# A long convolution by cosine and sine tables, split by the position modulo four instead of modulo two

## The chip, the core and the metric

The kernel runs on one core of a Trainium2 chip. Its engines work from queues of their own: TensorE (PE, the matrix products), VectorE (DVE), ScalarE (ACT), GpSimd (POOL) and SyncE (SP, which here issues the loads). They meet at semaphores. The metric is the device time of one execution in microseconds (us). Before the change it is 796.03 us, the median of 3 runs (793.9 to 798.8).

## The reference

One encoder layer on x (512 positions x 1024 channels): a mixer, a cross attention to 256 memory rows, and a mixture of 16 experts. The change is in the mixer, whose first half is a Hyena operator:

```python
def hyena_mixer(u, short_w, short_b, skip, k_f):       # u: 512 positions x 1536 channels
    u = conv_general_dilated(u, ...3 taps, per channel...) + short_b
    v, g1, g2 = jnp.split(u, 3, axis=-1)               # 512 channels each
    z = v
    for o, gate in enumerate((g1, g2)):
        zc = fft_long_conv(z, k_f[:, o]) + skip[o] * z
        z = gate * zc
    return z

def fft_long_conv(z, k_f):                             # z: 512 positions
    zf = jnp.fft.rfft(z, n=2 * L, axis=1)
    return jnp.fft.irfft(zf * k_f[None], n=2 * L, axis=1)[:, :L]

# in reference():
    h = rms_norm(x, norm_mix)
    u_hy, q, k, v = jnp.split(h @ w_in, split_at, axis=-1)
    k_f = hyena_filter_spectra(L, ...)                 # k2 / (sum |k2| + EPS), then rfft over 1024
    y_hy = hyena_mixer(u_hy, ..., k_f)
    y_at = gqa_mixer(q, k, v, ...)                     # 8 query heads, 2 key heads, rope
    y = concatenate([group_rms_norm(y_hy, ..., 8), group_rms_norm(y_at, ..., 8)])
    x = x + y @ w_out
```

## The kernel before

One program is written out by hand for each engine, in the order in which it runs; nothing reorders it. The stages: the filter of the convolution (a small network, then its spectra), the projections of x by `w_in`, the two convolutions, grouped attention in 32 steps with the end of the Hyena half between them, the output projection, the memory attention, and the experts.

**Products.** Where a product must be exact to nearly float32, both operands are split into a high and a low part (`_hi`, `_lo`), and PE makes three fast products (`hi*hi`, `hi*lo`, `lo*hi`). `chunk_jobs` (L1992) does so with the projections. The weights come in pieces of 512 KB: SP loads a piece into one of 3 slots (`w_raw`, `load_piece`) as soon as PE has used the piece three before it, ACT rounds it (`weight_hi`, L727, `w_hi`), and DVE takes the rest (`weight_lo`, L1165, `w_lo`). The chunks are `mk`, `mv` (memory keys and values), `v`, `g1`, `g2` (the three Hyena streams), `q` and `kv`, in that order.

**Transforms.** The spectrum of 512 positions zero-padded to 1024 is made by tables of cosines and sines. Positions of equal parity go through the same half-size table (`dft`), and even and odd results are then added and subtracted (`sums_and_differences`, L1242 and L1243). `spec_jobs` makes the spectra of the filters by full float32 products, `fwd_jobs` those of z by the three fast products, `inv_jobs` the way back by full float32 products, all with channels as the 512 columns of the spectra and time as the 512 columns (2 x 256) of the way back. So z is turned from channels-on-partitions to time-on-partitions by `z_jobs` (`zT`) before each convolution. `pointwise` (DVE) multiplies with the filter's spectrum: 20 operations on 128x512 for each half f of the spectrum and each order o. `skipped` (L1352) adds the skip term, scaled by the filter's l1 norm (`l1_norm`), and `gated` (L1359) multiplies with the gate. `outer_taps` (L1257 to L1260) and ACT's `centre_tap` (L739) make the 3-tap convolution.

**Fillers.** At five places PE makes products of the identity with itself, which nothing uses (`constant_products`, L1968), while it would wait for DVE or ACT.

**PSUM.** PE writes into 8 banks, and a bank is used again once its reader has freed it. `psum_jobs` lists all jobs in PE's order, and the banks are given out in turn.

**Order.** On PE: `filt(0)`, `mv`, spectra (order 0, with `filt(1)` between), `v`, spectra (order 1), `zT(0)`, `g1`, `fwd(0)`, `g2`, `inv(0)`, `zT(1)`, `fwd(1)`, `q`, `kv`, `inv(1)`, the keys' and first queries' transposes (`kT`, `qT`), and the scores of attention. On DVE, `weight_lo` calls stand between the operations of the stages.

Of the kernel before, what the change touches and what calls it, by code (L numbers as in the profile page):

```python
# [6 lines left out]
F32 = mybir.dt.float32  # L7
# [13 lines left out]
HALF = T // 2  # L21
NQ, NKV, HD = 8, 2, 64
# [37 lines left out]
GATED_STEP = 1  # L60
HN_STEPS = [8, 12]
MK_STEP = 9
# [5 lines left out]
FILL = [3, 3, 2, 2] + [1] * 6  # L68


def psum_jobs():
# [6 lines left out]
    def spec(o, f):  # L78
        return [("spec", o, f, c) for c in range(4)]
# [3 lines left out]
    jobs += spec(0, 0) + filt(1, (0, 1)) + spec(0, 1) + filt(1, (2, 3))  # L83
    jobs += [("u", c) for c in range(4)] + [("l1", 0)] + spec(1, 0) + spec(1, 1)
    jobs += [("zT", 0, k) for k in range(4)] + [("u", c) for c in range(4, 8)] + [("l1", 1)]
    for o in range(2):
        jobs += ([("zT", o, k) for k in range(4)] if o else []) + [("fwd", o, f, c) for f in range(2) for c in range(4)]
        jobs += [("u", c) for c in range(8, 12)] if o == 0 else [(key, i) for key in ("q", "kv") for i in range(TT)]
        jobs += [("inv", o, c) for c in range(CT)]
    jobs += [("kT", 0), ("kT", 1), ("qT", 0), ("qT", 1)]  # L90
    n = TT * NQ
    jobs += [("S", s) for s in range(AHEAD)]
    for s in range(-2, n):
# [12 lines left out]
        if s in HN_STEPS:  # L106
            jobs += [("hn", HN_STEPS.index(s))]
# [23 lines left out]
def build(nc, a, out, xn_dram, y_dram):  # L131
    with ExitStack() as ctx:
# [16 lines left out]
        rope_tmp = at("rope_tmp", 36, [P, 640])  # L149
# [15 lines left out]
        dft = at("dft", 104, [P, 2, 4, HALF])  # L165
        idft = at("idft", 112, [P, 2, 4, HALF])
        spec = at("spec", 120, [P, 2, 2, 4, CH])
        decay = at("decay", 152, [P, 4, CH])
        zt_hi = at("zt_hi", 152, [P, 4, CH], F32R)
        zt_lo = at("zt_lo", 32, [P, 4, CH], F32R)  # L170
        dft_hi = at("dft_hi", 24, [P, 2, 4, HALF], F32R)
        dft_lo = at("dft_lo", 104, [P, 2, 4, HALF], F32R)
        mk_sq = at("mk_sq", 160, [P, 512])
        q_sq = at("q_sq", 152, [P, TT, 512])
        ep = at("ep", 160, [P, 4, CH])
        mlp_arg = at("mlp_arg", 172, [FF, T])
        mlp_k = at("mlp_k", 174, [FF, T])
        l1sum = [at("l1sum0", 168, [P, CH]), at("l1sum1", 170, [P, CH])]
        fabs = [at("fabs0", 172, [P, 2, CH]), at("fabs1", 140, [P, 2, CH])]
        ab = at("ab", 168, [P, 4, CH])  # L180
        sum_diff0 = at("sum_diff0", 176, [P, 2, 4, CH])
        sum_diff = [sum_diff0, sum_diff1]
        sd = at("sd", 176, [P, 2, 4, CH])
        odd = at("odd", 192, [P, 2, CH])
# [4 lines left out]
        kT = at("kT", 88, [P, NKV, 2, T], F32R)  # L189
# [10 lines left out]
        inv_wide = at("inv_wide", 176, [P, TT, CT, 2, HD])  # L200
# [3 lines left out]
        y_sq = at("y_sq", 176, [P, CT, CH])  # L204
# [49 lines left out]
        blk = at("blk", 202, [P, P])  # L254
# [14 lines left out]
        for n, j in enumerate(jobs):  # L269
            if j[0] == "O":  # L270
                b = 6
            elif first_s < n < tail_s and j[0] in ("OT", "hn", "hr"):
                number[j] = len(number)
                b = 7
            elif j[0] == "gates":
# [38 lines left out]
        def open_bank(pe, job):  # L314

            b, use = place[job]
            if use:
# [3 lines left out]
                                          "dft", "idft", "x2", "g_moe", "wr")}  # L321
# [9 lines left out]
        s_skip = sem("skip_scaled")  # L331
# [20 lines left out]
        s_hrec = sem("hyena_inverse_ready")  # L352
        s_hwide = sem("hyena_inverse_wide")
# [7 lines left out]
        s_yh = sem("y_hyena_ready")  # L361
# [57 lines left out]
        def mat(name):  # L419
# [7 lines left out]
                  ("g2", w_in[:, :, 1024:1536], 2, [("u", c) for c in range(8, 12)]),  # L427
                  ("q", w_in[:, :, 1536:2048], 2, [("q", i) for i in range(TT)]),
                  ("kv", w_in[:, :, 2048:2304], 4, [("kv", i) for i in range(TT)]),
# [59 lines left out]
        def _(sp_):  # L489
# [21 lines left out]
            for n, m in ((1, ones), (2, blk), (3, tri)):  # L511
                sp_.dma_start(m[:], a["mats"][:, n, :]).then_inc(ld["mats"], 16)
# [155 lines left out]
        def _(act):  # L668
# [37 lines left out]
            def evac_odd(key):  # L706
                n = transforms.index(key)
                if n:
                    wait_freed(act, transforms[n - 1] + (1,))
# [1849 lines left out]
```

## Time and profile before

| | |
|---|---|
| median of 3 runs | 796.03 us (793.9 to 798.8) |
| the profiled execution, its span | 791.7 us |
| PE busy | 747.9 us, 94% of the span |
| DVE busy | 603.7 us, 76% |
| ACT busy | 461.6 us, 58% |
| share of the chain that ended last | PE 72%, DVE 15%, ACT 6% |
| filters, projections and convolutions | about 36 to 252 us |
| attention with the Hyena half's end | about 252 to 345 us |
| the rest (output projection, memory attention, experts) | 345 to 792 us |

The profiled execution has no time of its own beside its span; the median lies 4.3 us above the span. "Busy" is the time in which an engine had an instruction under way. PE's instructions overlap, so what one costs is read from the distance between two starts. A wait stands in square brackets behind the instruction that waited, with the engine that ended it.

### The profile page before, as it was taken

What the parts mean: (1) busy time and instruction counts of PE and PEld (TensorE: products, weight loads), DVE (VectorE), ACT (ScalarE), POOL (GpSimd) and SP (SyncE); (2) the same over time, 40 slices, a digit from 0 to 9 for tenths busy, and PEclk for the clock granted to TensorE, in tenths of its full rate; (3) what the DMA queues carried; (4) which work ended last, traced back from release to release, by engine and by line L of the source; (5) the groups of instructions that cost most, each with busy time, mean ns of one, the idle gap of its engine ahead of it and who ended that gap; (6) DMA issues with size and microseconds to landing.
All of it is one profiled execution on the core that took longest, in us unless ns stands there. A gap on an engine that the chain in (4) does not pass through costs nothing.

```text
span 791.7 us, 10886 instructions
## 1 busy us (share of the span) xinstructions
PE 747.9 (94%) x3680; PEld 607.8 (77%) x3680; DVE 603.7 (76%) x930; ACT 461.6 (58%) x689; POOL 78.0 (10%) x94
## 2 busy tenths in 40 slices
PE   5899999999999898889999999999999999999994
PEld 3664858788898787678787787888888888888882
DVE  5767482997799877835548568899899999999882
ACT  5952333131233988621559333787888888887782
POOL 0000000000000000000000001122222232222111
PEclk9999999999999999999999998999999999999997
DMA  8830203020120200022130675999999999999741
GB/s 291 298 107 1 84 23 106 27 80 1 38 96 27 78 31 1 2 62 97 54 116 18 246 294 182 420 364 385 379 372 383 373 391 372 369 369 383 306 159 21
DMA packets 28542, 146.53 MB, mean 185 GB/s; under 512 B 4791, under 2 KB 6711, under 8 KB 21976
## 3 DMA queue, kind: packets, MB, share of 16 engines
q1 hardware_dynamic: 23320, 135.53, 45.3%
q0 software_dynamic: 5184, 10.50, 5.0%
q8 instruction: 23, 0.38, 0.2%
q14 instruction: 15, 0.12, 0.0%
HBM read 141.81 MB, written 12.58 MB: 195 GB/s over the span
## 4 chain that ended last, share of the span: by engine, by line
PE 72%; DVE 15%; ACT 6%; DMA 4%; issue 3%; SPq 0%; POOL 0%; DVEq 0%; ACTq 0%; POOLq 0%
PE bank L1992 17%; PE bank L2378 11%; PE bank L2380 10%; PE bank L2379 10%; PE bank L1930 9%; PE bank L1937 3%; DMA slot<-in_w_down 2%; PE bank L2373 2%; PE bank L2004 1%; ACT w_hi L727 1%; PE bank L2292 1%; PE bank L2290 1%; PE bank L2291 1%; DVE w_lo L1165 1%; PE bank L2415 1%
## 5 line engine op out<-in xcount | busy, mean ns | idle before, releaser
L1849 DVE TENSOR_TENSOR e_lo<-slot,e_hi 128x1024 fp32r<-128x1024 f32 x192 | 221.4, 1218 | 9.4 <-ACT e_hi L1045 9.3
L1045 ACT ACTIVATE e_hi<-slot 128x1024 fp32r<-128x1024 f32 x192 | 188.2, 1061 | 7.7 <-DMA slot<-in_w_down 4.9
L1165 DVE TENSOR_TENSOR w_lo<-w_raw,w_hi 128x1024 fp32r<-128x1024 f32 x41 | 49.4, 1222 | 69.8 <-ACT w_hi L727 69.6
L727 ACT ACTIVATE w_hi<-w_raw 128x1024 fp32r<-128x1024 f32 x41 | 42.7, 1057 | 96.9 <-DMA w_raw<-in_w_in 63.2
L2378 PE MATMUL bank<-e_hi,hgT_hi 128*128 128x512 f32 x240 | 95.0, 396 | 0.3 <-DVE hgT_lo L1861 0.3
L2380 PE MATMUL bank<-e_hi,hgT_lo 128*128 128x512 f32 x240 | 93.6, 390 | 0.0
L2379 PE MATMUL bank<-e_lo,hgT_hi 128*128 128x512 f32 x240 | 93.4, 389 | 0.0
L2378 PEld LDWEIGHTS bank<-e_hi,hgT_hi 128*128 128x128 f32 x240 | 45.2, 189 | 9.5 <-DVE hgT_lo L1861 0.7
L2380 PEld LDWEIGHTS bank<-e_hi,hgT_lo 128*128 128x128 f32 x240 | 45.1, 188 | 9.6
L2379 PEld LDWEIGHTS bank<-e_lo,hgT_hi 128*128 128x128 f32 x240 | 45.1, 188 | 8.9
L2378 PE MATMUL bank<-e_hi,gaT_hi 128*128 128x512 f32 x120 | 48.1, 401 | 0.0
L2380 PE MATMUL bank<-e_hi,gaT_lo 128*128 128x512 f32 x120 | 46.9, 391 | 0.0
L2379 PE MATMUL bank<-e_lo,gaT_hi 128*128 128x512 f32 x120 | 46.8, 390 | 0.0
L1992 PE MATMUL bank<-hT_hi,w_hi 128*128 128x512 f32 x96 | 37.9, 395 | 0.0
L1992 PE MATMUL bank<-hT_lo,w_hi 128*128 128x512 f32 x96 | 37.4, 389 | 0.0
L1992 PE MATMUL bank<-hT_hi,w_lo 128*128 128x512 f32 x96 | 37.4, 389 | 0.0
L1992 PE MATMUL bank<-w_hi,hT_hi 128*128 128x512 f32 (+1 forms) x96 | 34.0, 354 | 0.8 <-DVE hT_lo L1171 0.8
L1992 PE MATMUL bank<-w_hi,hT_lo 128*128 128x512 f32 (+1 forms) x96 | 34.0, 354 | 0.0
L1992 PE MATMUL bank<-w_lo,hT_hi 128*128 128x512 f32 (+1 forms) x96 | 34.0, 354 | 0.0
L1063 ACT ACTIVATE hgT_hi<-bank 128x512 fp32r<-128x512 f32 x28 | 15.2, 596 | 31.1 <-PE bank L2373 31.1
L636 POOL DMA_INDIRECT out_dram<-eo,meta_i x16 | 25.4, 1588 | 76.7 <-ACT eo L1080 46.4
L1937 PE MATMUL bank<-ident,pr 128*128 128x128 f32 x160 | 24.8, 277 | 8.1 <-ACT pr L891 6.3
(395 smaller groups left out, 1671.6 us busy)
## 6 DMA issues: line engine op xcount, KB each, us to landing
slot<-in_w_down SPq DMA_DIRECT2D x16, 2048.0 KB, 16.6
slot<-in_w_gate SPq DMA_DIRECT2D x16, 2048.0 KB, 14.6
slot<-in_w_up SPq DMA_DIRECT2D x16, 2048.0 KB, 16.0
w_raw<-in_w_in SPq DMA_DIRECT2D x18, 512.0 KB, 3.5
w_raw<-in_w_out SPq DMA_DIRECT2D x8, 512.0 KB, 3.7
w_raw<-in_w_k_mem SPq DMA_DIRECT2D x4, 512.0 KB, 6.1
x_in<-in_x SPq DMA_DIRECT2D x4, 512.0 KB, 9.2
w_raw<-in_w_v_mem SPq DMA_DIRECT2D x4, 512.0 KB, 6.0
```

The lines of the kernel that those rows point to most:

```text
L636: pool.indirect_dma_start(out[0], bass.IndirectOffsetOnAxis(ap=meta_i[:, q, 0:1], axis=0), eo[q][:], None, bounds_check=T - 1, oob_is_err= ...
L727: act.activation(w_hi[ring(m)][:], w_raw[ring(m)][:], ACT.Copy).then_inc(s_wh, 1)
L1045: act.activation(e_hi[buffer(b, j)][:], slot[slot_][:, 1024 * part:1024 * (part + 1)], ACT.Copy).then_inc(s_ehi, 1)
L1165: dve.tensor_tensor(w_lo[slot_][:], w_raw[slot_][:], w_hi[slot_][:].bitcast(F32), ALU.subtract)\
L1849: dve.tensor_tensor(e_lo[slot_][:, at_], slot[slot_][:, at_], e_hi[buffer(b, j)][:].bitcast(F32), ALU.subtract)\
L1930: ins = pe.matmul(dst, l, r, start=(n == 0), stop=(n == len(pairs) - 1))
L1937: ins = pe.transpose(bank(job)[:, n * width:(n + 1) * width], s, ident[:])
L1992: ins = pe.matmul(bank(job)[:, 0:width], left, right, start=(k == 0 and m == 0), stop=(final and m == 2))
L2373: ins = pe.transpose(banks[half][:, k * P:(k + 1) * P], hg[q][:, c:D:KT], ident[:])
L2378: pe.matmul(dst, act_hi, w_hi_, start=first, stop=False)
L2379: pe.matmul(dst, act_hi, w_lo_, start=False, stop=False)
L2380: return pe.matmul(dst, act_lo, w_hi_, start=False, stop=last)
```

## The change

The positions are taken modulo four. The four residues have tables of 128 x 128 (`dft`: residue r, cosine or sine), a spectrum of 512 bins is made of 4 x 128 by two levels of sums and differences, and one stage does half of the channels (h, 256 of 512) instead of half of the bins. For residues 1 and 3, PE itself adds and subtracts: both products go into one bank, for the difference with a negated table (`dft_neg`, `turn_hi`, `turn_lo`). So PE's products of the transforms have 256 columns each instead of 512, and there are half as many columns in all for the way back, three quarters for the spectra and for `fwd`.

The way back now gives time on partitions, for residues 2rp and 2rp+1 in one bank. z stays with time on partitions, so `zT(1)` falls away; instead the gates are turned (`gT`, by `gate_jobs`, 16 transposes for each order), and ACT copies them to `gateT`. The skip term is put into the filter before its spectrum (`skip_added`, on one row, behind a product `l1_row` that sums the l1 terms over the partitions), and 1/l1 is put into the taps of the gate (`gate_taps`), so `skipped` falls away and `gated` is one product. `g2` now comes last of the projections, the stages lie in another order, three of the five fillers are gone, and `STAGE_BANKS` gives these jobs fixed banks (`filt` has 4 of them). The end of the Hyena half in attention (`hn`, `hyena_inverse`, `hyena_norm`) is done by reductions over the free axis on DVE. The rope gains are multiplied into the rope tables once. What follows attention is unchanged.

```diff
+STAGE_BANKS = {"filt": lambda o, t, way: (2 * t + way) % 4, "mv": lambda j: 4 + j, "l1row": lambda o: 7, "l1": lambda o: 6 + o,
+               "spec": lambda o, h, r: 4 + SPEC_ORDER.index(r), "fwd": lambda o, h, r: 4 + SPEC_ORDER.index(r),
+               "u": lambda c: c % 4, "q": lambda i: i, "kv": lambda i: i, "zT": lambda r: r,
+               "gT": lambda o, r: 6 + r % 2, "inv": lambda o, h, rp: 4 + 2 * h + rp, "kT": lambda j: 6 + j, "qT": lambda h: 6 + h}
...
             for t in range(4):
                 filters(0, t)
             weight_lo(7, 1)
-            l1_add(0, 0)
-            l1_add(0, 1)
+            for t in range(4):
+                l1_add(0, t)
             weight_lo(8, 3)
-            l1_add(0, 2)
-            l1_add(0, 3)
-            spec_sums(0, 0)
+            skip_added(0)
+            butterfly(("spec", 0, 0), spec[:, 0, 0])
...
+            def butterfly(key, dst):
+
+                sums, turned = key + (1,), key + (3,)
+                if key[0] == "fwd" and key != ("fwd", 0, 0):
+                    dve.wait_ge(s_ab, 2 * key[1] + key[2])
+                even_sums(key)
+                a_, b_ = (halves(first_level[:, n, :]) for n in range(2))
+                wait_filled(dve, sums)
+                c_ = halves(bank(sums)[:])
+                dve.tensor_tensor(pair(dst, 0, 4), a_, c_, ALU.add)
+                free(dve.tensor_tensor(pair(dst, 2, 4), a_, c_, ALU.subtract), sums)
+                wait_filled(dve, turned)
+                d_ = halves(bank(turned)[:])
+                dve.tensor_tensor(pair(dst, 1, 6), b_, d_, ALU.add)
+                free(dve.tensor_tensor(pair(dst, 3, 2), b_, d_, ALU.subtract), turned)
...
+            def spectrum(o, h):
+
+                x, k_, low = second_level, spec[:, o, h], inv_in[h]
+                butterfly(("fwd", o, h), x)
+                if o:
+                    wait_filled(dve, ("inv", 0, h, 1))
+                products = first_level[:].rearrange("p (g n) w -> p (g n w)", g=1).rearrange("p (b n) -> p b n", n=HC)
+                same = dve.tensor_tensor(products, x[:], k_, ALU.mult)
+                dve.tensor_tensor(low[:, 0:4], x[:, 0:4], k_[:, 4:8], ALU.mult)
+                link(dve.tensor_tensor(low[:, 4:8], x[:, 4:8], k_[:, 0:4], ALU.mult))
+                return products
+
+            def filtered(o, h, products):
+
+                y, low = second_level, inv_in[h]
+                dve.tensor_tensor(y[:, 0:4], products[:, 0:4], products[:, 4:8], ALU.subtract)
+                link(dve.tensor_tensor(y[:, 4:8], low[:, 0:4], low[:, 4:8], ALU.add))
...
+                dve.tensor_tensor(c_, y1, y3, ALU.add)
+                swapped_difference(first_level[:, 3, :], y1, y3)
+                dve.tensor_tensor(a_, y0, y2, ALU.add)
+                link(dve.tensor_tensor(b_, y0, y2, ALU.subtract))
+                second_sums(low, (3, 2), (1, 6)).then_inc(s_ab, 1)
...
+            made = spectrum(0, 0)
+            weight_lo(15, 1)
+            filtered(0, 0, made)
+            weight_lo(16, 1)
+            made = spectrum(0, 1)
+            outer_taps(4)
+            weight_lo(17, 1)
+            filtered(0, 1, made)
+            gated(0, 0)
...
+            made = spectrum(1, 0)
+            weight_lo(19, 2)
+            filtered(1, 0, made)
+            for i in range(TT):
+                wait_freed(dve, ("q", i))
+            roped(0)
+            weight_lo(21, 1)
+            made = spectrum(1, 1)
+            weight_lo(22, 1)
+            filtered(1, 1, made)
+            roped(1)
+            weight_lo(23, 1)
...
+            fwd_jobs(0, 0)
+            main_chunk("g1", slice(0, 1))
+            fwd_jobs(0, 1)
+            main_chunk("g1", slice(1, 4))
+            inv_jobs(0, 0)
+            main_chunk("q", slice(0, 1))
+            gate_jobs(0)
+            main_chunk("q", slice(1, 2))
+            inv_jobs(0, 1)
+            fwd_jobs(1, 0)
+            main_chunk("q", slice(2, 3))
+            fwd_jobs(1, 1)
+            main_chunk("q", slice(3, 4))
+            main_chunk("kv")
+            main_chunk("g2")
+            inv_jobs(1, 0)
...
             for h in range(2):
                 qT_job(h)
...
+            gate_jobs(1)
+            inv_jobs(1, 1)
```

The first place is DVE's queue between the filter's l1 sums and the first sums of the filter's spectrum (`w_lo` is a low part of weights, `l1sum` and `fabs` the l1 sums, `first_level` and `spec` results of the sums). Before:

```order
L1165 TENSOR_TENSOR w_lo_54<-w_raw_50,w_hi_58 128x1024
L1218 TENSOR_TENSOR l1sum_93<-fabs_95 128x512
L1220 TENSOR_TENSOR fabs_96<-fabs_96 128x512
L1221 TENSOR_TENSOR l1sum_93<-l1sum_93,fabs_96 128x512
L1165 TENSOR_TENSOR w_lo_55<-w_raw_51,w_hi_59 128x1024
L1165 TENSOR_TENSOR w_lo_53<-w_raw_49,w_hi_57 128x1024
L1165 TENSOR_TENSOR w_lo_54<-w_raw_50,w_hi_58 128x1024
L1220 TENSOR_TENSOR fabs_95<-fabs_95 128x512
L1221 TENSOR_TENSOR l1sum_93<-l1sum_93,fabs_95 128x512
L1220 TENSOR_TENSOR fabs_96<-fabs_96 128x512
L1221 TENSOR_TENSOR l1sum_93<-l1sum_93,fabs_96 128x512
L1242 TENSOR_TENSOR spec<-bank,odd 128x512
```

And with the change:

```order
L1271 TENSOR_TENSOR fabs_95<-fabs_95 128x512
L1272 TENSOR_TENSOR l1sum_89<-l1sum_89,fabs_95 128x512
L1271 TENSOR_TENSOR fabs_94<-fabs_94 128x512
L1272 TENSOR_TENSOR l1sum_89<-l1sum_89,fabs_94 128x512
L1271 TENSOR_TENSOR fabs_95<-fabs_95 128x512
L1272 TENSOR_TENSOR l1sum_89<-l1sum_89,fabs_95 128x512
L1216 TENSOR_TENSOR w_lo_55<-w_raw_51,w_hi_59 128x1024
L1216 TENSOR_TENSOR w_lo_53<-w_raw_49,w_hi_57 128x1024
L1216 TENSOR_TENSOR w_lo_54<-w_raw_50,w_hi_58 128x1024
L1281 SCALAR_TENSOR_TENSOR skip_add<-bank,skip_row 1x512
L1284 TENSOR_TENSOR sum_diff_107<-sum_diff_107,skip_add 1x512
L1322 TENSOR_TENSOR first_level<-bank,second_row 128x512
```

All four l1 terms now stand ahead of the three weight pieces, and the two operations on one row (`skip_added`) stand behind these.

The second place is PE's queue at the end of the convolutions, up to the first scores (`kT,qT`). Before:

```order
L1992 MATMUL bank<-w_hi_58,hT_hi 128x256
L1992 MATMUL bank<-w_lo_54,hT_hi 128x256
L1992 MATMUL bank<-w_hi_58,hT_lo 128x256
L1930 MATMUL bank<-idft,sd 128x256 x32
L1968 MATMUL bank<-ident 128x128 x16
L1937 MATMUL bank<-ident,k_split 128x128 x8
L1937 MATMUL bank<-ident,q_split 128x128 x8
L1930 MATMUL bank<-kT,qT 128x512 x6
```

And with the change (`u` are the gates of the second order, `inv_in` the way back's input of either half of the channels):

```order
L2105 MATMUL bank<-hT_hi,w_hi_58 128x512
L2105 MATMUL bank<-hT_hi,w_lo_54 128x512
L2105 MATMUL bank<-hT_lo,w_hi_58 128x512
L2043 MATMUL bank<-inv_in_108,idft 128x256 x8
L2081 MATMUL bank<-ident 128x128 x16
L2050 MATMUL bank<-ident,k_split 128x128 x8
L2050 MATMUL bank<-ident,q_split 128x128 x8
L2050 MATMUL bank<-ident,u 128x128 x16
L2043 MATMUL bank<-inv_in_109,idft 128x256 x8
L2043 MATMUL bank<-kT,qT 128x512 x6
```

Half of the way back and the 16 transposes of the gates now stand behind the keys' and queries' transposes, ahead of the first scores, and the chunk ahead of them is `g2` instead of `kv`.

## Rows read from the trace of the kernel before

**Rows 1.** The page: busy time, and the chain that ended last.

```profile
PE 747.9 (94%) x3680; PEld 607.8 (77%) x3680; DVE 603.7 (76%) x930; ACT 461.6 (58%) x689; POOL 78.0 (10%) x94
...
PE 72%; DVE 15%; ACT 6%; DMA 4%; issue 3%; SPq 0%; POOL 0%; DVEq 0%; ACTq 0%; POOLq 0%
```

**Rows 2.** Windows: length, busy time per engine, granted clock, DMA share, GB/s.

```profile
54.40:113.50 59.10, 58.95 (x202) 35.66 (x200) 37.24 (x61) 21.12 (x29) 0.00 (x0) 1.00 0.15 45
113.50:252.00 138.50, 137.03 (x688) 116.28 (x686) 110.22 (x191) 37.73 (x59) 0.00 (x0) 1.00 0.17 54
...
262.00:345.00 83.00, 73.55 (x523) 64.54 (x522) 61.94 (x126) 61.65 (x133) 4.73 (x7) 1.00 0.09 33
```

**Rows 3.** Timeline of PE, 169 to 256 us: start, duration, instructions, wait.

```profile
171.17 2.39 PE L1968 MATMUL bank<-ident 128*128 128x128 f32 x20
173.94 14.08 PE L1930 MATMUL bank<-idft,sd 128*128 128x256 f32 x64 [0.38 <-DVE sd L1344]
187.86 1.72 PE L1968 MATMUL bank<-ident 128*128 128x128 f32 x14
...
191.45 1.95 PE L1968 MATMUL bank<-ident 128*128 128x128 f32 x16
...
251.70 3.73 PE L1968 MATMUL bank<-ident 128*128 128x128 f32 x32
```

**Rows 4.** Groups of PE, 36 to 262 us: operation, count, busy, mean ns.

```profile
L1930 PE MATMUL bank<-sum_diff,dft 128*128 128x512 f32 x64 | 28.1, 595 | 0.2 <-DVE spec L1243 0.2
```

**Rows 5.** Timeline of PE: products of 512 columns, then of 256.

```profile
226.14 0.39 PE L1992 MATMUL bank<-w_hi,hT_lo 128*128 128x512 f32 x1
226.37 0.28 PE L1992 MATMUL bank<-w_hi,hT_hi 128*128 128x256 f32 x1
226.48 0.28 PE L1992 MATMUL bank<-w_lo,hT_hi 128*128 128x256 f32 x1
```

**Rows 6.** Timeline of DVE: first and last operation of one stage, and what follows.

```profile
147.88 0.68 DVE L1242 TENSOR_TENSOR ab<-bank,odd 128x512 f32<-128x512 f32 x1
...
160.27 1.22 DVE L1165 TENSOR_TENSOR w_lo<-w_raw,w_hi 128x1024 fp32r<-128x1024 f32 x1
```

**Rows 7.** Groups of DVE, 40 to 262 us, shapes kept apart.

```profile
L1165 DVE TENSOR_TENSOR w_lo<-w_raw,w_hi 128x1024 fp32r<-128x1024 f32 x21 | 25.3, 1221 | 40.0 <-ACT w_hi L727 39.9
...
L1257 DVE SCALAR_TENSOR_TENSOR u<-bank,cols,u 128x256 f32<-128x256 f32 x12 | 5.7, 475 | 0.0
...
L1352 DVE SCALAR_TENSOR_TENSOR u<-u,small,bank 128x512 f32<-128x512 f32 x8 | 5.7, 742 | 0.8 <-PE bank L1930 0.8
```

**Rows 8.** Timeline of PE: the filter's products, and the first spectrum.

```profile
38.72 1.02 PE L2004 MATMUL bank<-w_diff,a 128*128 128x512 f32 x2
...
54.40 1.88 PE L1930 MATMUL bank<-sum_diff,dft 128*128 128x512 f32 x4
```

**Rows 9.** Timeline of DVE, 36 to 62 us.

```profile
41.67 4.87 DVE L1211 TENSOR_TENSOR sum_diff<-bank,decay 128x512 f32<-128x512 f32 x8
50.26 1.22 DVE L1165 TENSOR_TENSOR w_lo<-w_raw,w_hi 128x1024 fp32r<-128x1024 f32 x1 [3.73 <-ACT w_hi L727]
...
57.36 3.50 DVE L1165 TENSOR_TENSOR w_lo<-w_raw,w_hi 128x1024 fp32r<-128x1024 f32 x3 [3.82 <-ACT w_hi L727]
```

**Rows 10.** Timeline of DVE into attention.

```profile
253.73 2.28 DVE L1454 TENSOR_REDUCE small<-q_sq 128x32 f32<-128x2048 f32 x1
255.92 2.72 DVE L1352 SCALAR_TENSOR_TENSOR u<-u,small,bank 128x512 f32<-128x512 f32 x4
...
258.94 0.69 DVE L1491 TENSOR_REDUCE small<-bank 128x1 f32<-128x512 f32 x1
```

**Rows 11.** Windows of PE alone, experts' stage: length, busy time, granted clock.

```profile
468.00:471.40 3.40, 2.79 (x23) 1.00 0.98 313
471.50:474.80 3.30, 3.30 (x9) 0.50 1.07 457
...
485.00:492.00 7.00, 6.67 (x21) 0.51 0.31 90
```

More of the change, by code:

```diff
@@ L21 @@
 HALF = T // 2
+NR = 4
+RM = T // NR
+HC = CH // 2
+SPEC_ORDER = (2, 0, 1, 3)
 NQ, NKV, HD = 8, 2, 64
@@ L1295, in _ @@
-            z_lo(0)
-            for k in range(2):
-                dve.wait_ge(s_dhi, k + 1)
-                dve.tensor_tensor(dft_lo[:, k], dft[:, k], dft_hi[:, k].bitcast(F32), ALU.subtract).then_inc(s_dlo, 1)
-            weight_lo(15, 3)
+            filters(1, 3)
+            for t in range(4):
+                l1_add(1, t)
+            dve.wait_ge(ld["rows"], 16)
+            dve.wait_ge(ld["rope"], 16)
+            dve.wait_ge(s_gq, 1)
+            skip_added(1)
+            weight_lo(11, 1)
@@ L1382, in _ @@
-            pointwise(0, 0)
-            weight_lo(19, 1)
-            pointwise(0, 1)
-            weight_lo(20, 2)
-            outer_taps(8)
-            for c in range(CT):
-                skipped(0, c)
-                gated(0, c)
-            z_lo(1)
-            weight_lo(22, 1)
-            pointwise(1, 0)
-            weight_lo(23, 1)
-            pointwise(1, 1, (24,))
-            dve.wait_ge(ld["rows"], 16)
-            dve.wait_ge(ld["rope"], 16)
-            dve.wait_ge(s_gq, 1)
@@ new lines, in quarter, with gated @@
+            def quarter(buf, h, rp):
+                return buf[:, 2 * rp:2 * rp + 2, h * HC:(h + 1) * HC]
+            def gated(o, h):
+                for rp in range(2):
+                    job = ("inv", o, h, rp)
+                    wait_filled(dve, job)
+                    for r in (2 * rp, 2 * rp + 1):
+                        wait_freed(dve, ("gT", o, r))
+                    g = quarter(gateT[o], h, rp)
+                    ins = dve.tensor_tensor(g, halves(bank(job)[:]), g, ALU.mult)
+                    ins.then_inc(s_z, 1)
+                    link_free(job)
@@ L1454, in _ @@
             dve.tensor_reduce(small[:, 240:272], q_sq[:].rearrange("p i (h d) -> p (i h) d", d=HD), AX.X, ALU.add).then_inc(s_ms, 1)
-            for c in range(CT):
-                skipped(1, c)
+            outer_taps(8)
+            gated(1, 0)
+            gated(1, 1)
             dve.wait_ge(s_hrms, 3)
             dve.reciprocal(small[:, 240:272], small[:, 240:272]).then_inc(s_qinv, 1)
-            def hyena_inverse():
-                dve.wait_ge(s_hroot, 1)
-                dve.reciprocal(small[:, 280:312], small[:, 280:312]).then_inc(s_hrec, 1)
```

745 lines of the change are left out of this document (396 added, 349 removed).

## The prediction

> **What bounds the kernel now.** I read the page first: PE is busy 94% of the span, DVE 76%, and the last chain is 72% PE [rows 1]. A mean does not say where DVE stands, so the windows came next. From 54.4 to 113.5 us PE is busy 58.95 of 59.10 us, from 113.5 to 252 us 137.03 of 138.5, while DVE has 37.24 and 110.22 [rows 2]. In the second window DVE is thus at 80%: it can take little more. PE's timeline shows that three of its busy stretches are fillers, 2.39, 1.72 and 1.95 us [rows 3], so PE already waits 6.1 us there for DVE or ACT, out of sight. DVE's groups show the other side: 40.0 us of its idle time ends with ACT's high part of weights [rows 7]. These run in a ring of three slots: PE uses a piece, SP loads the next into its place, ACT rounds it, DVE subtracts, PE goes on. Extra DVE work in front of a subtraction becomes a PE wait.
>
> **The change, in three legs.** The sum is made against the profiled span, 791.7 us; the median is 4.3 us above it.
>
> *Prices.* Full float32: 28.1 us for 32 products of 512 columns (64 records), 0.88 each [rows 4]; 14.08 us for 32 products of 256, 0.44 each [rows 3]. Fast products: 0.23 us for 512 columns, 0.12 for 256, start to start [rows 5]. A transpose or filler: 0.12 us [rows 3]. DVE: a stage's 20 operations take 12.39 us, 0.60 each and some 0.1 more where one waits for the one before [rows 6]; 1024 columns 1.14 us each (three in 3.50) [rows 9]; 2048 columns 2.28 us [rows 10]; a tap on 256 columns 0.48 us [rows 7].
>
> *Leg A, to the end of zT (113.5 us).* The filters' spectra fall from 28.1 us to 48 x 0.44 = 21.1, the two l1_row products add 1.8, the l1 products of order 1 come here from the next leg (+0.9, 8 records of 0.11 as the fillers [rows 3]): -4.3 us. New waits:
> - filt has 4 banks instead of 8. The fourth product ends near 39.7 us [rows 8]; the fifth needs the bank that DVE frees with its first operation, at 41.67 + 0.7 [rows 9]: 2.7 us.
> - l1_row needs all l1 sums. They stand behind weight_lo(7), which starts at 50.26 us [rows 9] and now 2.7 later, since its load waits for PE; with 7 sums at 0.72 they end near 59.2. PE is through mv at 54.4 [rows 8] + 2.7: 2.1 us.
> - skip_added stands behind the three pieces of weights (57.36 + 3.50 [rows 9], again 2.7 later) and two one-row operations, so until 65.0; PE has done l1_row and one spectrum by 61.1: 3.9 us.
> - The same for order 1, where DVE is further ahead: estimated 0.8 us. zT now follows v at once and waits for the last taps (three operations of 512, near 0.7 each [rows 7]): 2.1 us.
>
> Together 11.6 - 4.3 = +7.3; I take +7, zT ending at 120.5.
>
> *Leg B, to the first kT (before: 251.70 + 3.73 = 255.4 us [rows 3]).* PE loses: fwd from 96 x 0.23 to 144 x 0.12, -4.5; of inv three quarters remain here, 28.1 to 10.5, -17.6; three fillers, -6.1; l1, -0.9. gT(0) replaces zT(1) one for one. PE's own work falls from some 140.4 us (137.03 busy [rows 2] and 3.4 of the last filler) to 111.3, so alone it would reach kT at 232.
>
> DVE does not let it. One stage is now 6 sums of 512 (3.6), a product of 2048 (2.3), four operations of 1024 (4.6), 3.5 of 512 (2.3), four of 512 (2.4), and six links (0.6): 15.8 to 16.3 us instead of 12.4, four times. DVE's bill from z_lo to the last taps: stages 64.4, 11 pieces of weights 13, z's low parts 4.9, taps on 8 channels 11.1 (two of 511 columns instead of four of 256 [rows 7]), gated with its one-element copies 3.2, memory sums 2.9, rope gains and rope 14.7, splits 3.1, sum of squares 2.3 (each by its operations at the prices above): 119.6 us. Two pieces of weights still come too late for it (the first two stages end before load and rounding are through; at most the 3.8 us of a wait shown in [rows 9] each): 5.5. So 125 us from 121.5, to 246.5. g2 is the last projection and its low parts stand near the end of this queue; its taps take the last 5.5 us, hence g2 ends near 242.3 on PE, then half of inv(1), 3.5, and the remaining filler, 3.7 [rows 3]: kT at 249.5, 5.9 us earlier than before. Inside the leg that is some 18 us of PE waits, mostly ahead of pieces of q, kv and g2 whose low parts stand behind a stage on DVE (2 to 5 us each).
>
> *Leg C, into attention.* Before, DVE went from its last sum to skipped (2.72 us) and to the first row maximum at 258.94 [rows 10], with kT and qT beside it: 3.5 us after kT's start. Now kT and qT (1.9), gT(1) (1.9, and some 2.7 of waits for ACT to copy, two banks for four jobs), inv(1,1) (3.5), the last gated and the reciprocal (1.1) stand in a row: 11.1 us, so the first maximum comes at 260.6: +1.7 in all.
>
> *Attention.* The 16 small products of hn go (two records of 0.11 each, as the fillers [rows 3]: 3.6 us of PE); in their place DVE sums the squares, and ACT takes one square root for all, ahead of a piece of weights that PE waits for. Between -3.6 and +5.0 (one more wait of 3.8 and a piece of 1.2 [rows 9]) I take -1, since PE has 9 us of waits in this stage already [rows 2]. After it nothing changes.
>
> *What costs nothing.* ACT is busy 37.73 of 138.5 us in the second window [rows 2], so its new copies (gates, squares of the keys) and the half of the evacuations that it loses change nothing. SP issues decay and dft in four parts each and a skip row of single elements ahead of a piece of weights; that lies before the filter and is covered by it; uncovered it is one more wait of at most 3.7 us [rows 9]. The load of x2 now waits for the last gated; its first reader is the output projection, behind all of attention, so 80 us cover it.
>
> *The clock.* In this kernel PE is nearly never idle before 252 us and keeps the full level [rows 2]. Where it is idle the granted clock falls: a stretch with 2.79 us busy of 3.40 is followed by one at 0.50, and another at half level lasts 7 us though PE is busy 6.67 of them [rows 11]. At 1.2 instead of 2.4 GHz, 3.3 us of full work lose 1.65. New idle lies close together near 57 to 65, 117 to 124, 210 to 225 and 250 to 255 us. Nothing lost is one end; four stretches of 1.65 to 3.3 us, 13 us, the other. A part falls where DVE sets the pace and costs nothing: +4.
>
> *Sum:* 1.7 - 1 + 4 = +4.7, span 796.4, median **801 us**. The 28 us of PE work come back as waits.
>
> **Rivals.**
> 1. *The saved columns arrive.* If DVE's long operations in SBUF ran at twice the rate per column, a stage would lose (2.3 + 4.6)/2 = 3.4 us, four stages 14; PE would be the bound again and the time about 787. Against it: 1024 columns cost 1.14 us, 2048 cost 2.28, just in proportion to 0.60 for 512 [rows 6, 9, 10]. Or the loads come soon enough that leg A loses nothing: then 794. Chance 0.13 for the two together, of which most for times under 788.
> 2. *Slower: the clock.* The idle stretches keep PE at half level while PE itself is the pace (leg A and leg C, where nothing hides it). It decides as soon as more than two of the four stretches fall; the upper end, 13 instead of 4, gives 810. For it: the half level of 7 us at full work [rows 11]; against it: from 262 to 345 us PE is busy 73.55 of 83 us and keeps 1.00 [rows 2]. Chance 0.25.
> 3. *Slower: dearer forms.* DVE reads two blocks of 256 from PSUM and writes strided pairs; with the 0.74 of L1352 [rows 7] in place of 0.60 for the 12 such operations of a stage it is +6.7 us, 808. Chance 0.12.
>
> The Trainium skill ("TensorE: Matmul & The Clock Gate", Part 1: The HAM clock gate) says that "the default state is throttled, and activity releases the throttle"; by that rule taking fillers out speaks against this change, and the sum would be nearer to the second rival's 810. The trace agrees so far as it shows a fall behind idle time [rows 11]; which of the new waits suffice, no row shows.
>
> **Numbers.** Forecast 0.5, rivals 0.13, 0.25, 0.12. The forecast's own range is 795 to 806; with rivals 2 and 3 at 808 to 810 and a part of rival 1, 790 to 811 holds eight in ten. A difference of 1% is about what a measurement here can tell: under 788.1 faster 0.12, over 804.0 slower 0.36 (rivals 2 and 3, and the forecast's upper edge), between them 0.52.
>
> **What would show it.** PE waits of 2 to 4 us at 39.7, 57, 61 and 117 us; zT ending at 120.5; stages of 16 us on DVE; DVE without idle time to speak of from 121 to 246; kT near 249.5; the first maximum near 260.6; the clock at half level behind the four stretches. Wrong would be: DVE idle again for long in leg B (then PE or the loads are the bound), stages under 14 us, or a difference that arises after 345 us, where no instruction changes.

## The result: 2.0% slower, and the profile after

| | before | after |
|---|---|---|
| median, in the same comparison (4 runs each) | 797.41 us (793.9 to 799.3) | 811.54 us (809.65 to 813.12) |
| ratio, 95% interval | | 1.0196 [1.0156, 1.0236] |
| span of the profiled execution | 791.7 us | 808.4 us |

The forecast was 801 us with a range of 790 to 811. The time is 0.5 us outside it, and slower where no change was called likeliest. PE has less to do, as reckoned, and the time is longer all the same. The medians lie 14.1 us apart and the spans of the two profiled executions 16.7; executions of one kernel differ by some us, and what follows is read from one of each. From the page of the kernel after, as [rows 1]:

```profile
PE 732.8 (91%) x3634; PEld 606.0 (75%) x3634; DVE 615.2 (76%) x910; ACT 465.0 (58%) x693; POOL 78.3 (10%) x94
```

PE is busy 15.1 us less, in 16.7 us more. PE's busy time also holds stretches in which the granted clock stood at its lower level, 1.2 GHz instead of 2.4 (0.50 in the windows below; "half level" from here on, and a "fall" is such a stretch), so its columns fell by more than that. The windows from zT's end to kT and on to the first row maximum answer to [rows 2]:

```profile
129.20:260.80 131.60, 117.19 (x624) 102.34 (x625) 115.10 (x163) 36.89 (x58) 0.00 (x0) 0.94 0.19 57
260.80:272.60 11.80, 9.52 (x56) 8.18 (x55) 3.59 (x9) 6.03 (x11) 0.00 (x0) 1.00 0.01 1
```

The same leg of before, from zT's end to kT:

```profile
113.70:255.30 141.60, 140.12 (x716) 119.38 (x715) 113.32 (x194) 38.08 (x58) 0.00 (x0) 1.00 0.17 53
```

In leg B, where PE had 1.5 us of idle time, it now has 14.4. DVE's 115.10 us are close to what it had (113.32). The granted clock is no longer 1.00 there.

PE's timeline shows the waits one by one, in brackets at the end of a row:

```profile
43.97 1.14 PE L2118 MATMUL bank<-w_sum,a 128*128 128x512 f32 x2 [4.02 <-DVE sum_diff L1262]
...
63.50 1.02 PE L2126 MATMUL bank<-l1sum,ones 128*32 128x512 f32 x2 [2.22 <-DVE l1sum L1272]
...
68.94 1.02 PE L2147 MATMUL bank<-sum_diff,dft 128*128 128x256 f32 x2 [3.36 <-DVE sum_diff L1284]
...
125.51 3.66 PE L2050 MATMUL bank<-ident,u 128*128 128x128 f32 x16 [2.36 <-DVE u L1353]
...
168.29 0.76 PE L2105 MATMUL bank<-w_hi,hT_hi 128*128 128x512 f32 x1 [2.39 <-DVE u L1353]
...
202.96 0.50 PE L2105 MATMUL bank<-w_hi,hT_hi 128*128 128x512 f32 x1 [2.01 <-DVE w_lo L1216]
...
224.44 0.50 PE L2105 MATMUL bank<-hT_hi,w_hi 128*128 128x512 f32 x1 [3.56 <-DVE w_lo L1216]
...
235.22 0.80 PE L2105 MATMUL bank<-hT_hi,w_hi 128*128 128x512 f32 x1 [5.05 <-DVE w_lo L1216]
...
260.82 1.04 PE L2050 MATMUL bank<-ident,k_split 128*128 128x128 f32 x8
...
300.88 1.09 PE L2050 MATMUL bank<-ident,pr 128*128 128x128 f32 x4 [5.14 <-ACT pr L942]
```

In PE's timeline of before, zT and kT:

```profile
111.81 1.91 PE L1937 MATMUL bank<-ident,u 128*128 128x128 f32 x16
...
255.27 1.04 PE L1937 MATMUL bank<-ident,k_split 128*128 128x128 f32 x8
```

The waits were forecast nearly to the place and the size: 4.02, 2.22, 3.36 and 2.36 us for 2.7, 2.1, 3.9 and 2.1 in leg A, and 2 to 5 us ahead of pieces of weights in leg B. The transposes of zT, 16 in 3.66 us at 125.51, show what was not: before, they took 1.91 us. They run at the half level. Windows of PE alone (length, busy time, granted clock) around such places:

```profile
45.00:48.50 3.50, 3.50 (x6) 0.53 0.00 0
69.00:72.50 3.50, 3.50 (x9) 0.52 0.00 0
123.50:129.00 5.50, 3.49 (x16) 0.52 0.18 70
129.00:134.50 5.50, 4.65 (x24) 0.55 0.00 0
168.00:172.00 4.00, 3.71 (x10) 0.57 0.00 0
233.00:240.00 7.00, 4.78 (x12) 0.51 0.03 11
...
297.00:304.50 7.50, 3.62 (x17) 0.55 0.00 0
334.30:338.50 4.20, 3.15 (x13) 0.63 0.02 4
```

Seven stretches at 1.2 GHz lie between 36 and 345 us (the third and fourth row are one), each at a wait of PE; in the profile of before, the first lies at 471 us. Summed over windows of 1 us as busy time times the missing part of the clock, they take 14.6 us of PE. An eighth, at 14 to 22 us, lies ahead of all that the change touches: the filter starts at 36.24 us, and at 36.04 before without it. DVE's timeline closes the picture:

```profile
128.00 2.52 DVE L1394 TENSOR_TENSOR zt_lo<-bank,zt_hi 128x512 fp32r<-128x512 f32 x4
...
195.77 0.68 DVE L1339 TENSOR_TENSOR second_level<-first_level,bank 128x512 f32<-128x512 f32 x1
196.37 0.68 DVE L1340 TENSOR_TENSOR second_level<-first_level,bank 128x512 f32<-128x512 f32 x1
197.08 2.29 DVE L1436 TENSOR_TENSOR first_level<-second_level,spec 128x2048 f32<-128x2048 f32 x1
199.29 1.22 DVE L1437 TENSOR_TENSOR inv_in<-second_level,spec 128x1024 f32<-128x1024 f32 x1
...
255.63 1.41 DVE L1353 SCALAR_TENSOR_TENSOR u<-bank,cols,u 128x511 f32<-128x511 f32 x2
...
267.24 0.69 DVE L1465 TENSOR_TENSOR gateT<-bank,gateT 128x512 f32<-128x512 f32 x1 [10.20 <-ACT gateT L805]
...
272.64 0.69 DVE L1604 TENSOR_REDUCE small<-bank 128x1 f32<-128x512 f32 x1
```

The long forms cost what was taken for them (2.29 and 1.22 us), z_lo to the last taps is 129.0 us (forecast 125), and the first row maximum, at 258.94 before [rows 10], comes at 272.64. Leg by leg, with the forecast beside it:

| us | forecast | measured |
|---|---|---|
| leg A, zT's end (before 111.81 + 1.91) | +7 | 129.17 - 113.72 = +15.5 |
| leg B, to kT (before 255.27) | -12.9 | 131.65 - 141.55 = -9.9 |
| leg C, to the first maximum | +7.6 | 11.82 - 3.67 = +8.2 |
| attention and the rest | -1 | 535.8 - 532.8 = +3.0 |
| the clock | +4 | in the lines above |
| sum | +4.7 | +16.7 |

### The profile page after: what moved, and what is told of

Read it like the earlier page. It is cut to its first block, busy times and chain, and to the rows that moved or that the text cites. A ratio compares the mean times of both kernels' runs of the same rounds, so it can differ in the third digit from the quotient of the medians.

```text
span 808.4 us, 10814 instructions
## 1 busy us (share of the span) xinstructions
PE 732.8 (91%) x3634; PEld 606.0 (75%) x3634; DVE 615.2 (76%) x910; ACT 465.0 (58%) x693; POOL 78.3 (10%) x94
## 4 chain that ended last, share of the span: by engine, by line
PE 70%; DVE 13%; ACT 8%; DMA 5%; issue 3%; SPq 0%; POOL 0%; DVEq 0%; ACTq 0%; POOLq 0%
PE bank L2105 16%; PE bank L2524 10%; PE bank L2526 10%; PE bank L2525 10%; PE bank L2043 8%; PE bank L2050 3%; DMA slot<-in_w_down 2%; PE bank L2519 2%; DVE w_lo L1216 2%; PE bank L2118 2%; DMA w_raw<-in_w_v_mem 1%; ACT w_hi L762 1%; ACT pr L1046 1%; PE bank L2081 1%; DMA w_raw<-in_w_in 1%
## 5 line engine op out<-in xcount | busy, mean ns | idle before, releaser
L2050 PE MATMUL bank<-ident,pr 128*128 128x128 f32 x160 | 25.6, 284 | 12.0 <-ACT pr L942 10.2
L2050 PEld LDWEIGHTS bank<-ident,pr 128*128 128x128 f32 x160 | 18.9, 144 | 18.3 <-ACT pr L942 13.7
```

Source lines behind the costliest of these rows:

```text
L2050: ins = pe.transpose(bank(job)[:, n * width:(n + 1) * width], s, ident[:])
```

## The experiments

Theory C: the queues go as reckoned, and what is above the sum is mostly the half level behind PE's new waits. Theory D: DVE sets the pace, and the half level lies in time that is lost anyway. The times stand with the ratio to the kernel before on the same chip, whose median was 794.0 to 795.7 us in the experiments and 797.41 us beside the changed kernel. So a difference of two runs is read from the ratios; between raw medians the changed kernel looks 2 to 3 us worse than it is.

| | median us | ratio to before, 95% | first row maximum |
|---|---|---|---|
| changed kernel | 811.54 | 1.0196 [1.0156, 1.0236] | 272.64 |
| e1 fillers | 804.81 | 1.0115 [1.0075, 1.0155] | 266.99 |
| e2 DVE short | 803.22 | 1.0101 [1.0062, 1.0139] | 264.43 |
| e3 before, no fillers | 797.68 | 1.0046 [1.0019, 1.0073] | 262.08 |
| e4 filter, 8 banks | 806.22 | 1.0140 [1.0100, 1.0180] | 267.11 |
| e5 root later | 810.66 | 1.0183 [1.0139, 1.0226] | 273.16 |
| e6 skip row later | 809.39 | 1.0169 [1.0122, 1.0216] | 274.00 |
| e7 residues on DVE | 813.13 | 1.0234 [1.0191, 1.0278] | 274.15 |
| e8 gates before keys | 806.61 | 1.0147 [1.0108, 1.0185] | 268.54 |
| e9 waits removed | 784.86 | 0.9868 [0.9841, 0.9896] | 247.76 |
| e10 the same, fillers | 785.40 | 0.9866 [0.9841, 0.9892] | 247.60 |
| e11 fillers to zT | 806.75 | 1.0165 [1.0146, 1.0183] | 269.25 |
| e12 fillers after zT | 811.18 | 1.0215 [1.0193, 1.0237] | 270.66 |

**e1, e11, e12: fillers in the waits.** PE makes products of the identity with itself where it would be idle.

```diff
+                        if (o, t, way) == (0, 2, 0):
+                            constant_products(("mv", 0), 16)
                         open_bank(pe, job)
...
+                constant_products(("fwd", 0, 0, 2), 10)
                 for c in range(CT):
                     wait_freed(pe, ("u", c))
...
+            constant_products(("kT", 0), 14)
+            main_chunk("g2", slice(0, 1))
+            constant_products(("kT", 0), 20)
+            main_chunk("g2", slice(1, 4))
```

> The changed kernel with products of the identity put into seven of PE's new waits (16 before the fifth filter product, 9 before l1_row, 14 before the first spectrum that needs the skip term, 10 and 12 around zT, 10 before q, 14 and 20 before the first two pieces of g2), about as long as the waits. Theory C (the clock): the waits themselves were forecast rightly, and some 10 us on top are half-level stretches behind them; the falls at 45, 69, 124, 168 and 232 us go, the first row maximum comes at 261 to 264 instead of 272.6, and the time is 799 to 804 us. Those in attention (297, 334) stay. Theory D (DVE alone sets the pace, the half level lies in time that is lost anyway): 809 to 814.

> The changed kernel with the fillers of e1 up to zT and the first fwd only (16, 9, 14, 10 and 12 products of the identity); none ahead of q and g2. Where the half level counts: if it counts only where PE sets the pace (leg A, where DVE waits for PE as well), this gives all that e1 gave: 803 to 806. If it counts everywhere alike, three of five falls go: 806 to 808. If e1 gained by something else than the clock: 810 to 813.

> The changed kernel with the fillers of e1 ahead of q and of the first two pieces of g2 only (10, 14 and 20). If the half level counts only where PE sets the pace: no gain, 810 to 813, though the falls at 168 and 233 us are gone. If it counts everywhere alike: two of five falls go, 807 to 809.

In e1 PE keeps the full level up to kT; two falls lie behind it, one of them new (260 to 264 us). PE's timeline of e1, zT and kT:

```profile
122.90 2.17 PE L2050 MATMUL bank<-ident,u 128*128 128x128 f32 x16
...
253.61 1.04 PE L2050 MATMUL bank<-ident,k_split 128*128 128x128 f32 x8
```

From the windows of PE of e1, over the places of five falls:

```profile
40.00:49.00 9.00, 7.70 (x44) 1.00 0.05 20
66.00:74.00 8.00, 7.79 (x41) 1.00 0.00 0
122.00:135.00 13.00, 12.98 (x98) 1.00 0.01 1
160.00:172.00 12.00, 11.78 (x69) 1.00 0.19 59
216.00:241.00 25.00, 23.56 (x131) 1.00 0.21 64
```

In the changed kernel the granted clock is 0.81, 0.79, 0.61, 0.86 and 0.86 in the same windows. zT ends 4.1 us earlier, kT starts 7.2 us earlier, and the first maximum comes 5.65 us earlier, at 266.99 us where 261 to 264 was expected: leg C, with the new fall in it, takes 1.6 us back. The ratio falls from 1.0196 to 1.0115 (the intervals lie just apart). Products that nothing uses made the kernel faster, which theory D excludes; 804.8 is just above the range that theory C gave. It is no pure gain: the fillers outlast some of the waits, and mv ends at 60.24 us instead of 61.12 (its last product's start plus 0.23). e11 and e12 were measured beside each other: fillers up to zT alone give 806.75, those behind it alone 811.18, no better than none, though the falls at 168 and 233 us are gone (a shorter one comes at 201, and one behind kT). Their forecasts do not agree on a rule: e11 lies in the range of "everywhere alike", e12 in that of "only where PE sets the pace", and e11's ratio is still inside the interval of the changed kernel. What holds is that e11 is 0.5% faster than e12, with intervals apart. In the profiles leg A is 4.2 us shorter in e11 and leg B 2.8 us shorter in e12, and both move the first maximum, by 3.4 and 2.0 us. So the half level counted in leg A; in leg B it counted in the profiles of e1 and e12 and not in e12's median, and that stays open.

**e2: less of DVE.**

```diff
-                same = dve.tensor_tensor(products, x[:], k_, ALU.mult)
+                same = dve.tensor_tensor(products[:, 0:1], x[:, 0:1], k_[:, 0:1], ALU.mult)
...
-                dve.tensor_tensor(y[:, 0:4], products[:, 0:4], products[:, 4:8], ALU.subtract)
-                link(dve.tensor_tensor(y[:, 4:8], low[:, 0:4], low[:, 4:8], ALU.add))
+                dve.tensor_tensor(y[:, 0:1], products[:, 0:1], products[:, 1:2], ALU.subtract)
+                link(dve.tensor_tensor(y[:, 4:5], low[:, 0:1], low[:, 4:5], ALU.add))
```

> Leaves out seven eighths of the products with the real part of the filter's spectrum and three quarters of the sums that follow, in each of the four stages: some 3.5 us of DVE less each, 14 us in all, so that a stage costs DVE about what it did before the change. Theory D: DVE sets the pace of the whole leg from zT to the keys' transposes, 14 us less there: 797 to 800. Theory C: about 9 us of PE's waits in that leg go, leg A and its falls of the clock stay: 801 to 806. If PE and the clock alone set the pace: 809 to 812.

803.22: some 8 of the 14 us arrive, as theory C said. The waits ahead of the taps and the weights shrink or go (PE's timeline of e2, the rows that answer to 224.44 and 235.22):

```profile
216.75 0.50 PE L2105 MATMUL bank<-hT_hi,w_hi 128*128 128x512 f32 x1 [0.98 <-DVE w_lo L1216]
225.94 0.50 PE L2105 MATMUL bank<-hT_hi,w_hi 128*128 128x512 f32 x1 [3.45 <-DVE w_lo L1216]
```

DVE's longer stage is a real cost in leg B; the rest of the gap to before, 1.0%, is not the length of these stages.

**e3: the kernel before without its three fillers.**

```diff
-                            constant_products(("zT", 1, 0), 7)
+                            constant_products(("zT", 1, 0), 0)
...
-                                constant_products(job, 8)
+                                constant_products(job, 0)
...
-                    constant_products(("inv", 0, 0), 10)
+                    constant_products(("inv", 0, 0), 0)
```

> The kernel before without the three fillers that the change takes out (7, 8 and 10 products of the identity). Theory C: PE waits there instead of filling, as long as before; if such short idle time near 170 to 193 us is enough for a fall, one stretch at half level, 798 to 801; if not, 795 to 798. Theory D: no difference, 795 to 798, and no fall of the clock that matters.

797.68 against 794.64 us, 0.5% slower. The median lies 0.3 us inside the range that both theories gave for no fall that matters; the interval leaves no doubt of the sign. Waits turned into falls. A row of PE's timeline of e3:

```profile
195.18 0.65 PE L1930 MATMUL bank<-zt_hi,dft_hi 128*128 128x512 f32 x1 [1.98 <-DVE zt_lo L1293]
```

And windows of PE of e3 behind the two places:

```profile
174.50:178.50 4.00, 4.00 (x13) 0.57 0.00 0
195.00:199.00 4.00, 3.82 (x10) 0.57 0.02 4
```

The fillers that the change took out were worth 3 us to the kernel before (1.5 to 5.8 by the interval). The profile's rows of before could not show it: there they are busy time that ends within 0.4 us of the operand. The attention of e3, whose code is that of before, has falls at 287 and 325 us where the profile of before has none: such a fall can come in one execution and not in another.

**e4 and e6: the wait in the filter.** e4 gives the first order's filter products 8 banks. e6 moves one load.

```diff
-"filt": lambda o, t, way: (2 * t + way) % 4, "mv": lambda j: 4 + j
+"filt": lambda o, t, way: (2 * t + way) % (4 if o else 8), "mv": lambda j: j
```

```diff
                 load_piece(n)
+                if n == NSLOT + 3:
+                    sp_.dma_start(skip_row[:].rearrange("o a (c p) -> o (a c) p", p=P),
...
```

> The changed kernel with 8 banks for the first order's filter products, as before the change (mv then takes the first two). The wait of 4.02 us ahead of the fifth product goes. Theory C: with it goes the fall at 45 us (1.8 us lost): 804 to 807. Theory D or a hidden wait: 807.5 if only the wait counts, 810 to 813 if leg A is covered by something else, the loads of weights above all.

> The changed kernel with the load of the skip row (1024 single elements) behind the first mv pieces on SP's queue instead of ahead of them. If it is what makes mv's weights late: SP issues the mv pieces some 4 us earlier, w_hi starts at 37.2 us instead of 38.4, PE's wait at the fifth filter product is 2.7 instead of 4.02, the time 809.5 to 811. If the four-part loads of dft and decay are to blame: no change of that wait, 811 to 812.

e4: 806.22, as theory C had it, though 807.5 for the wait alone is too near to be told apart; mv ends at 55.59 instead of 61.12 us with no fall ahead of it (one of 11 us follows at 58), so leg A is a chain that is paid for. e6 settles a smaller point. SP's queue in the changed kernel (start, time in the queue, what is loaded):

```profile
25.07 0.79 SPq L549 DMA_DIRECT2D skip_row<-in_cols  x1
25.89 3.72 SPq L552 DMA_DIRECT2D rows<-in_rows  x1
...
30.61 0.94 SPq L519 DMA_DIRECT2D w_raw<-in_w_v_mem  x2
```

The same queue in e6:

```profile
25.20 0.60 SPq L549 DMA_DIRECT2D rows<-in_rows  x1
...
26.80 1.19 SPq L519 DMA_DIRECT2D w_raw<-in_w_v_mem  x2
```

And PE's wait at the fifth filter product in e6:

```profile
42.73 2.08 PE L2119 MATMUL bank<-w_sum,a 128*128 128x512 f32 x2 [2.65 <-DVE sum_diff L1263]
```

Behind the row of single elements the next load holds the queue for 3.72 us, so mv's weights are issued 3.8 us later, and the fifth product starts 1.2 us later (43.97 us against 42.73); without it the wait is 2.65 us, the 2.7 of the forecast. The time hardly moves, and mv ends at 61.01 us, as late as in the changed kernel: the half level now covers all four products (the window from 42.5 to 49 us has a clock of 0.50). That the shorter wait brought this is not shown: in e2 and e8, whose code up to here is that of the changed kernel, it covers them too, behind waits of 3.52 and 5.28 us.

**e5: the square root in attention.**

```diff
-Y_ROOT_STEP = 8
-Y_NORM_STEP = 10
+Y_ROOT_STEP = 13
+Y_NORM_STEP = 14
```

> The changed kernel with ACT's square root for the Hyena half's norm at step 13 of attention, where it was before the change, instead of step 8, where it meets a copy of kT, one of oT and a piece of weights; norm and row transposes follow later. Theory C: PE's wait of 5.14 us at 300.88 falls to about 2, as before the change, and the half level behind it goes: 807 to 809. Theory D (attention is paced by DVE and ACT anyway, the wait moves elsewhere): 810.5 to 813.

The wait falls from 5.14 to 2.09 us as expected, and the stretch from the first maximum to the first product of the output projection from 75.7 to 73.6 us (72.2 before). A fall of the clock stays (298 to 302 us), and the median, 810.66, tells nothing: the expectation of 807 to 809 missed. Nor do the 2 us of the stretch tell much: it is 74.05 us in e6 with the root at step 8, and 75.48 in e10 with it at step 13.

**e7: residues 1 and 3 on DVE again.** A third row of the spectrum is copied by ACT, and DVE adds and subtracts.

```diff
+                    dve.tensor_tensor(first_level[:, 2, :], bank(sums)[:], third_row[:], ALU.add)
+                    free(swapped_difference(first_level[:, 3, :], halves(bank(sums)[:]), halves(third_row[:])), sums)
...
-                        if r == 3:
-                            terms = pairs(1, c) + pairs(3, c, minus)
-                        elif r == 1:
-                            terms = pairs(1, c) + pairs(3, c)
```

> Undoes one part of the change: in fwd the sums and differences of residues 1 and 3 are made on DVE again (one copy on ACT, two 512-column sums on DVE more for each stage), PE makes half as many products for them and needs no negated table: PE loses 48 x 0.12 = 5.8 us, DVE gains some 1.4 us for each of four stages. If PE sets the pace of that leg: 805 to 807. If DVE does alone (theory D): 815 to 818. Theory C, in which both take turns: 811 to 814, and PE's waits in the leg grow by 6 to 7 us.

813.13, within theory C's 811 to 814. PE makes 48 products less, 5.8 us by their price, and its waits take that back: 6.30 us ahead of the piece of q where the changed kernel has 2.01, 3.99 where it has 2.39. So the sums on PE by a negated table are neither the loss nor a gain that this comparison can tell.

**e8: gates ahead of the keys.**

```diff
-    jobs += [("kT", 0), ("kT", 1), ("qT", 0), ("qT", 1)] + gate(1) + inverse(1, 1)
+    jobs += gate(1) + inverse(1, 1) + [("kT", 0), ("kT", 1), ("qT", 0), ("qT", 1)]
```

> The changed kernel with gT(1) and the second half of inv(1) ahead of the keys' and queries' transposes, and without the 16 fillers there. From the sum of leg C: DVE's gating runs beside the transposes, the first row maximum comes 4 to 5 us earlier: 806 to 808. Rival: kT and qT are what the scores wait for, so only the filler's 3.7 us less what it covered: 810 to 812.

806.61: the first maximum 4.1 us earlier although zT, behind the same code, ends 2.2 us later in this profile. Leg C was sized right.

**e9 and e10: the causes of the waits removed.** e4, e6 and e8 together with the root at step 13, skip_added ahead of the three pieces of weights, the memory keys' sums in leg A, and weight_lo(15) behind the first stage:

```diff
-            weight_lo(8, 3)
             skip_added(0)
+            weight_lo(8, 3)
...
-            weight_lo(15, 1)
             filtered(0, 0, made)
-            weight_lo(16, 1)
+            weight_lo(15, 1)
             made = spectrum(0, 1)
+            weight_lo(16, 1)
```

> The changed kernel with the causes of its waits taken away: 8 banks for the first filter products, the skip row loaded behind mv's first pieces, skip_added ahead of the three pieces of weights, the memory keys' sums of squares in leg A (where DVE waits) instead of leg B, weight_lo(15) behind the first stage, gT(1) and inv(1,1) ahead of kT, the square root at step 13. Laid side by side by the durations of the trace, the queues end 16 to 17 us earlier than the changed kernel's. Theory C: 795 us if the half level costs the same 10 to 12 us as before, 790 to 799 with more or fewer falls. Theory D: the gains in leg A are swallowed by leg B's DVE bill: 802 to 806.

> The same, with products of the identity in five of the waits that are left (9 ahead of l1_row, 9 and 13 around zT, 15 and 21 ahead of the first two pieces of g2). The queues' end is not moved by them. Theory C: the falls near 55, 115 and 210 us go, 5 to 8 us less than without: 784 to 791, faster than both kernels. Theory D: the same time as without fillers, within 2 us.

784.86 us, 1.3% faster than before and, by the two ratios, 3.2% than the changed kernel; better than theory C's 790 to 799. Against the changed kernel leg A is 10.2 us shorter in the profile, and legs B and C together 14.7. Of the 3.3 points between the ratios, e4, e5, e6 and e8 make 1.5 by themselves; the three moves that no run makes alone, or what the moves do together, make the rest. Four falls are left ahead of kT, and fillers (e10) take them away without any gain. Windows of PE of e9:

```profile
57.00:61.00 4.00, 3.81 (x8) 0.57 0.25 95
115.00:119.00 4.00, 3.54 (x16) 0.57 0.00 0
204.00:211.00 7.00, 5.24 (x12) 0.51 0.16 59
```

The same windows of e10:

```profile
57.00:61.00 4.00, 3.26 (x13) 1.00 0.30 111
115.00:119.00 4.00, 4.00 (x35) 1.00 0.02 4
204.00:211.00 7.00, 6.79 (x37) 1.00 0.14 56
```

Here theory D is right and C wrong: e10's time lies within C's 784 to 791, but the 5 to 8 us between the two runs did not come. zT ends 1.9 us earlier with fillers (117.11 for 119.02), but its low part, which the first fwd waits for, starts only 0.5 us earlier on DVE, in e9 and in e10:

```profile
117.95 2.46 DVE L1402 TENSOR_TENSOR zt_lo<-bank,zt_hi 128x512 fp32r<-128x512 f32 x4
117.43 2.47 DVE L1402 TENSOR_TENSOR zt_lo<-bank,zt_hi 128x512 fp32r<-128x512 f32 x4
```

The first maximum stands at 247.60 for 247.76: DVE's queue sets it.

## Why the prediction was wrong

- **What bounds the kernel, the prices, the ring: right.** Stages of 16 us on DVE, 2.29 and 1.22 us for the long forms. Rival 1 fell by that (no operation ran at twice the rate, and leg A did lose), rival 3 too: the sums of 512 in two blocks start 0.60 us apart. Two slips in the working change nothing: 96 x 0.23 to 144 x 0.12 is -4.8 and not -4.5, and 3.5 operations of 0.60 are 2.1 and not 2.3 (the trace has 2.6).
- **The waits: right** in place and nearly in size, but for the first: 4.02 for 2.7 us. The step "SP ... is covered by it" failed there: 1.3 us of the wait, of the 3.7 that were allowed, are gone without the skip row (2.65 in e6). PE's waits in leg A are 13.2 us together instead of 11.6.
- **Legs B and C: right in kind.** DVE shows 11.0 us of waits between z_lo and the last taps instead of 5.5. The two pieces of weights take just the 5.5 (4.30 and 1.22 us); what the sum lacked is 3.2 for the first fwd, which runs at the half level, 2.0 for products of the way back and 0.35 for ACT's centre tap. Leg C +8.2 for +7.6.
- **Attention: +3.0 instead of -1, and the sign is not shown.** The one square root meets two copies and a piece of weights on ACT, a wait of 5.14 us, close to the upper end of 5.0, and e5 takes it down to 2.09. But from the first maximum to the end it is 532.8 us in the profile of before and 536.1 in e3 with the same code there, and 534.4 to 538.3 in the nine profiles with the changed kernel's attention.
- **The clock: the term that was mis-sized.** The step was "four stretches ... A part falls where DVE sets the pace and costs nothing: +4". The trace shows five falls ahead of kT and two in attention. Those of leg A stand in PE's chain: 1.7 us in the filter, 1.7 in the spectrum, 1.8 on zT (3.66 for 1.9 us), 5.2 of the 8.5 by which leg A was missed. e11, with fillers there, ends zT 4.2 us earlier; e1, without the five, starts kT 7.2 us earlier, 5.65 of which are left at the first maximum. So by these two profiles the half level ahead of kT alone cost about 7 us where 4 were allowed for all of it, and leg A's part is already those 4. The second rival named this mechanism and 810 us, and had 0.25; it should have been the likeliest case, since [rows 11] show falls that last, and leg A opens four waits on PE with nothing to hide what follows them. Its second half (leg C) was not seen: no fall lies there.
- **What stays open.** The spans miss the sum by 12.0 us (8.5 in leg A, 3.0 in B, 0.6 in C and 4.0 in attention, less the 4 allowed for the clock), the medians by 9.4. The half level ahead of kT, 7.2 us in e1, is 3 more than was allowed, and the longer first wait is 1.3. No run separates the rest: attention, whose profiles of one code differ by 4 us, what the two falls there cost (3.5 us of PE, and no fillers were tried there), and about 1.7 us of leg A.

The Trainium skill ("TensorE: Matmul & The Clock Gate", Part 1: The HAM clock gate) says that the default state is throttled and that activity releases the throttle. e1, e3 and e11 agree: products that nothing uses keep the full level. e10 adds a limit to what that is worth: nothing in the time where another engine sets the pace.

## What to carry to other kernels

Where a change moves work from PE to DVE, write down which engine each stretch waits for, and price every wait that opens on PE twice: once as the wait, and once as the half level behind it if PE is the pace there. Fillers in a profile can be hidden waits, as the three of e3 were, so a change that removes them has to look first at what they covered. An order of queues can be worth more than the arithmetic: the same transforms went from 2.0% slower to 1.3% faster than before (e9) by giving out banks otherwise and moving one load, two operations on one row, the memory keys' sums, some pieces of weights, the last gates, and the square root in attention. And a stretch of a few us is compared over several executions before a cause is given for it.

## What the runs showed that was not expected

- The half level outlasts the idle time by far: from 123.5 to 134.5 us the clock is 0.52 to 0.55 while PE is busy 8.1 of 11 us.
- A load of 1024 single elements held SP's queue for the load behind it: 3.72 us for `rows`, which takes 0.60 without it (e6); in five more runs with that order it is 3.5 to 4.5 us.
- Falls are not the same in every execution. At the filter the changed kernel's code has one from 45 to 49 us in its own profile, from 42 to 50 in e2 and from 44 to 51 in e8. In e3 waits of 1.68 and 1.98 us, with 1.94 us of transposes between them, were followed by a fall; in attention before, waits of 1.86 and 1.68 us some 6.8 us apart by none, and in e3 the same code has two falls there. No rule for when a fall comes is shown.
